# Moving the first attention step's scores and softmax into the last values chunk of the layer

## The reference

```python
def diff_attention(q, k, v, lam):
    s = jnp.einsum('bqahd,bkahd->bahqk', q, k).astype(jnp.float32) * (B_QK_DIM ** -0.5)
    p = jax.nn.softmax(s, axis=-1)
    a = (p[:, 0] - lam * p[:, 1]).astype(v.dtype)
    return jnp.einsum('bhqk,bkhe->bqhe', a, v)
```

## Time and profile before

| what | value |
|---|---|
| runs of the kernel | 3079.67 us median of 3 (3075.52 to 3081.51) |
| profiled execution | 3081.39 us, its span 3079.6 us |
| instructions | 51919 |
| TensorE matmuls | 2942.7 us busy, 96% of the span |
| TensorE weight loads | 2705.6 us, 88% |
| VectorE | 1056.2 us, 34% |
| ScalarE | 1522.4 us, 49% |
| GpSimd | 2176.1 us, 71% |
| mean granted TensorE clock | 0.966 of full speed |
| memory read, written | 488.86 MB, 3.15 MB |

### The profile page before, as it was taken

How to read it: one execution, slowest core, us unless ns; L and a number is a source line. 1 busy time by engine, 2 the same in 40 slices (tenths; PEclk the granted TensorE clock), 3 DMA queues, 4 the chain that set the end, 5 groups by cost and what they waited for, 6 DMA issues and landing times.

```text
span 3079.6 us, 51919 instructions
## 1 busy us (share of the span) xinstructions
PE 2942.7 (96%) x21842; PEld 2705.6 (88%) x21842; DVE 1056.2 (34%) x1979; ACT 1522.4 (49%) x2005; POOL 2176.1 (71%) x912
## 2 busy tenths in 40 slices
PE   7999989999999999989999999899999999999998
PEld 7877969988877879979899999787899989789998
DVE  2412422123214221031563433225634342464433
ACT  4665454446565454444564444444654444465443
POOL 6667697886667788866566886565586867557686
PEclk9999999999999999989999999899999999999999
DMA  6445455564445455544344554443354554334454
GB/s 217 144 151 171 145 196 174 185 202 154 151 151 176 159 179 185 181 156 155 134 151 158 172 179 152 163 138 112 130 167 148 178 180 157 131 124 156 149 179 147
DMA packets 136521, 495.39 MB, mean 161 GB/s; under 512 B 15072, under 2 KB 17760, under 8 KB 135136
## 3 DMA queue, kind: packets, MB, share of 16 engines
q1 hardware_dynamic: 131904, 480.53, 46.6%
q10 hardware_dynamic: 4384, 11.54, 1.1%
HBM read 488.86 MB, written 3.15 MB: 160 GB/s over the span
## 4 chain that ended last, share of the span: by engine, by line
PE 83%; ACT 6%; DVE 4%; DVEq 2%; POOL 1%; ACTq 1%; issue 1%; DMA 0%; SPq 0%
PE lin L464 17%; PE lin L465 17%; PE lin L466 17%; PE aux L464 4%; PE aux L466 4%; PE aux L465 4%; PE aux L557 2%; PE lin L490 2%; PE lin L491 2%; PE lin L492 2%; ACT whi L1003 2%; POOL wlo L443 1%; PE aux L626 1%; PE aux L898 1%; PE aux L842 1%
## 5 line engine op out<-in xcount | busy, mean ns | idle before, releaser
L443 POOL TENSOR_TENSOR wlo<-raw,whi 128x1024 fp32r<-128x1024 f32 x908 | 2175.9, 2412 | 887.9 <-ACT whi L1003 887.1
L1003 ACT ACTIVATE whi<-raw 128x1024 fp32r<-128x1024 f32 x908 | 949.6, 1057 | 982.1 <-PE lin L466 723.5
L464 PE MATMUL lin<-in_hi,whi 128*128 128x256 f32 x3968 | 1146.7, 289 | 25.2 <-POOL wlo L443 22.4
L465 PE MATMUL lin<-in_lo,whi 128*128 128x256 f32 x3968 | 1127.9, 284 | 0.0
L466 PE MATMUL lin<-in_hi,wlo 128*128 128x256 f32 x3968 | 1127.3, 284 | 0.0
L464 PEld LDWEIGHTS lin<-in_hi,whi 128*128 128x128 f32 x3968 | 766.6, 193 | 63.7 <-issue 52.8
L465 PEld LDWEIGHTS lin<-in_lo,whi 128*128 128x128 f32 x3968 | 767.0, 193 | 0.7
L466 PEld LDWEIGHTS lin<-in_hi,wlo 128*128 128x128 f32 x3968 | 766.2, 193 | 0.0
L464 PE MATMUL aux<-br_hi,whi 128*128 128x256 f32 x880 | 250.7, 285 | 7.6 <-DVE br_lo L1418 7.6
L465 PE MATMUL aux<-br_lo,whi 128*128 128x256 f32 x880 | 250.3, 284 | 0.0
L466 PE MATMUL aux<-br_hi,wlo 128*128 128x256 f32 x880 | 250.2, 284 | 0.0
(11 more groups left out here) (240 smaller groups left out, 3679.7 us busy)
## 6 DMA issues: line engine op xcount, KB each, us to landing
raw<-in_wstream SPq DMA_DIRECT2D x908, 512.0 KB, 3.3
Z<-in_rel ACTq DMA_DIRECT2D x2, 1536.0 KB, 7.1
Z<-in_mem_t ACTq DMA_DIRECT2D x2, 1024.0 KB, 7.8
kv_store<-Z ACTq DMA_DIRECT2D x2, 1024.0 KB, 7.0
Z<-kv_store ACTq DMA_DIRECT2D x2, 1024.0 KB, 11.2
x<-in_x_t SPq DMA_DIRECT2D x1, 1024.0 KB, 4.9
Z<-in_ctx_t SPq DMA_DIRECT2D x1, 1024.0 KB, 4.8
out_x<-x SPq DMA_DIRECT2D x1, 1024.0 KB, 3.9
```

Source lines behind the costliest of these rows:

```text
L443: pool.tensor_tensor(wlo[s][:, :], raw[s][:, :], whi[s][:, :].bitcast(F32), ALU.subtract).then_inc(lo_pool, 1)
L464: pe.matmul(out, wh, xh, start=start, stop=False, skip_group_check=True)
L465: pe.matmul(out, wh, xl, start=False, stop=False, skip_group_check=True)
L1003: act.activation(whi[s][:, :], raw[s][:, :], ACT.Copy).then_inc(hi_ready, 1)
```

## The change

On TensorE the scores of step 0 are issued behind the second unit (index 1) of the last values chunk, instead of after the chunk. The wait for `qk_done` goes with them. In the layer of `x` whose context keys come from memory (`stored`), they also wait for `kv_landed`, which the wait for `values_ready` covered. The wait for `values_ready` moves ahead of the first product with the values, in `diff_values(0)`. On ScalarE, lambda's two exponentials move from behind the second values chunk to behind the first, then come three of the second chunk's four conversions, the exponentials of step 0, the fourth conversion and the copy of the chunk. VectorE's program stays as it is. It applies to all three passes.

```diff
@@ diff_values (TensorE)
                 if tt == 0 and t.ahead(yb_taken, 0):
                     pe.wait_ge(yb_taken, t.ahead(yb_taken, 0))
+                if n == 0:
+                    pe.wait_ge(values_ready, t.next(values_ready))
                 pe.wait_ge(pt_ready, t.next(pt_ready))
@@ second_layer (TensorE)
-            def second_layer(kts, rotate):
+            def second_layer(kts, rotate, stored=False):
+                def first_scores():
+                    pe.wait_ge(qk_done, t.ahead(qk_done, 0))
+                    if stored:
+                        pe.wait_ge(kv_landed, t.next(kv_landed, 32))
+                    diff_scores(0, kts)
+
                 rms()
...
-                token_chunk(1)
-                pe.wait_ge(qk_done, t.ahead(qk_done, 0))
-                pe.wait_ge(values_ready, t.next(values_ready))
+                token_chunk(1, after={1: first_scores})
                 fill = second_fill()
-                diff_scores(0, kts)
                 for n in range(STEPS):
...
-            for _ in range(L):
-                second_layer(4, True)
+            for l in range(L):
+                second_layer(4, True, l == 1)
@@ second_layer (ScalarE)
                 values_chunk(0, zt(v, 4), qk_roots)
-                values_chunk(1, zt(v + 4, 4))
+                act.wait_ge(lam_sum, t.next(lam_sum))
+                act.activation(small[:, 18:20], small[:, 16:18], ACT.Exp).then_inc(lam_exp, 1)
+                hi_parts(3)
+                diff_exps(0, kts)
+                evacuate(1, 1, zt(v + 4, 4))
                 act.drain()
                 if rotate and l == 1:
                     act.wait_ge(kv_landed, t.next(kv_landed, 32))
                 act.drain().then_inc(values_ready, 1)
-                act.wait_ge(lam_sum, t.next(lam_sum))
-                act.activation(small[:, 18:20], small[:, 16:18], ACT.Exp).then_inc(lam_exp, 1)
                 fill = second_fill()
-                diff_exps(0, kts)
                 for n in range(STEPS):
```

## The result

| | time, median (range) | ratio to the kernel before, 95% interval |
|---|---|---|
| before | 3079.03 us (3073.73 to 3081.51, 5 runs) | |
| changed | 3060.53 us (3048.79 to 3068.35, 5 runs) | 0.9939 [0.9921, 0.9957] |

The change takes 18.5 us off and comes to 3060.53 us, where 3062.5 was forecast.

The account below looks back on a forecast made before the run. TensorE, busy 96%, sets the pace, so time is won only where it idles or runs at half clock. 7.4 + 8.7 + 2.7 = 18.8 us off the profiled 3081.39 gives 3062.6, taken as 3062.5; range 3056 to 3069.

Parts of the forecast that it names:

- The first gap: TensorE's idle time between the last values chunk and step 0's scores: 2.45 us in each of three passes, 7.4 removed.
- the second: TensorE's lost time between step 0's scores and its transposes: 2.31, 3.03 and 3.37 us, together 8.7 us removed.
- The clock: TensorE at half clock on scores, unit and transposes in the second pass only: 2.7 us removed.
- The added part: Cost of the new order in three queues: no stall taken; bounds nothing to 1.6 us for each 512-key pass.
- The wait for the keys and for the transfer: TensorE's early scores need the last keys, done 9.6 us earlier, and an 11.2 us transfer issued some 80 us ahead: nothing.
- Lambda's load: ScalarE's table load and exponential behind the first values chunk delay the next conversion by at most 1.5 us, covered.
- The chain: Softmax of step 0, from scores to probabilities: 6.3 us bare, ready 0.3 us before TensorE comes 9.5 us after the scores' start.
- the hold of the ratio's product: Tiny VectorE product in step 0's softmax, held by GpSimd's low-half operation from 2643.1 to 2643.7.
- A late softmax: VectorE waits under GpSimd leave part of the idle time before the transposes: at most 3.5 us, 3066; chance 0.12.
- The starving queue: ScalarE's conversion and PSUM freeing stand behind late exponentials, so TensorE waits for weights: slower, 3086; chance 0.03.
- The rival of the moved wait: Line 1346's wait is not what ended the idle time before the scores; only the later idle time goes: 3070; chance 0.03.
- The clock gave 5.65 us back: Rival: shifted idle spots downstream lose the clock more often, five new losses of 2.7 us, about 3076; chance 0.04.

Follow-up runs that it names:

- the first experiment: Kernel before with TensorE's scores right behind the whole values chunk, not waiting for the stored values, ScalarE's order unchanged: 3083.79 us against 3077.05, ratio 1.002.
- The two later comparisons: The changed kernel itself, run again against the kernel before: ratio 0.9926 (3053.89 us), then 0.9925 (3058.47 us against 3081.66).
- the placing behind the third unit: Changed kernel with the scores of step 0 behind the third unit (index 2) of the last values chunk instead of the second: 3065.58 us, one execution.
- the last experiment: Changed kernel with VectorE's fill work moved from in front of the next step's maxima to behind them: 3052.42 us, ratio 0.9895 to the kernel before.
- the other deal: Changed kernel with the second fill unit before the values moved from steps 5, 9, 13 to 4, 8, 12: 3060.24 us, ratio 0.9952 to the kernel before.

## Why the prediction was right

**The first gap, 7.4 us, and the second, 8.7.** Together 16.1 were forecast; 15.7 are gone. The sum was right, but the two terms are not independent savings, as the rival in the first experiment would have it: done one by one, the parts do not bring their terms. Moving the wait alone brought 0.0 us, moving lambda alone 2.3, moving both with the exponentials ahead of the copy, but still at the chunk's end, 5.9. The rest, 9.8 us, is the cover of two more units. The prediction did not say this; it added the gaps because the change undoes both at once. The scores at their early place with ScalarE's old order were not tried.

**The clock, 2.7 us.** By the second transposes 18.6 us are gone, so the clock's part is 2.9, of which the second pass has 2.8. The Trainium skill's rule ("TensorE: Matmul & The Clock Gate", "HAM oscillation"), that idle gaps between bursts bring back the half clock, would have given up to two more such losses. The profiled execution of before does not show them, but the runs elsewhere side with the rule more than the prediction did: the same gap at the chunk's end (2.68, 3.21, 3.55 us) lost the clock in all three passes, and with lambda alone moved the gap ahead of the scores (2.29 us) lost it in two of three. The 2.7 us thus rest on a loss that one profiled execution happened to show once; that they came out at 2.9 says that this loss is gone, and not how often the kernel before has it. The two later comparisons gave 21.9 and 23.2 us instead of 18.5; that executions of before lose the clock there more often than the one profiled did would fit, and is not shown.

**The added part, nothing.** The wait for the keys and for the transfer: no wait of line 898 in any pass. Lambda's load: in the third pass the conversion behind it came late (it starts at 2625.30, 0.7 us after its unit by the distance of the others), no TensorE wait follows. The chain: forecast ready 0.3 us before TensorE, measured 0.30; the hold of the ratio's product under GpSimd forecast to 2643.7 of the old time, 0.6 us long, measured 0.68. In the context's pass the last VectorE operation ends 0.83 us before the transposes. The rule on the shared port ("SBUF — State Buffer", "SBUF: two separate sides", of the Trainium skill) held each time. In the profile of the changed kernel 43 VectorE products on 128x1 or 128x2 numbers began inside a GpSimd operation that had over 0.2 us to run, and each ended 0.01 to 0.02 us behind it.

**The rivals.** A late softmax did not come; the placing behind the third unit shows how near it was. What the prediction held against it, that steps with two units of cover show no gap, does not hold as it stands: steps 5, 9 and 13 have two units and are the ones that wait, up to 2.88 us at step 5; the last experiment shows VectorE's backlog as a cause at step 5. The starving queue was tested and did not come. The rival of the moved wait had line 1346 not ending the first gap; the first experiment shows that it did end it, since the scores came at once without that wait, but that the time then went to the second gap. The clock gave 5.65 us back in one profiled execution, in a stretch ahead of the change, and 4.6 in another, most of it behind the attention steps; the medians of the three comparisons all show 18.5 us or more gained.

**What was thin.** The range, 3056 to 3069, held the median, but single runs of the changed kernel spread from 3048.8 to 3068.4, wider than the three runs of before had shown; a median of few runs could have fallen below it, as that of a later comparison did (3053.89).

## What to carry to other kernels

When an engine waits twice in a row, ask whether the two waits are links of one chain: if they are, take the first away alone and the second grows by as much, as it did here. A chain is shortened by reordering the engine that runs it, and covered by starting it earlier on the engine that waits; count every queue it passes, the conversion ahead of it and the holds included, and compare the sum with the cover in tenths of a microsecond. Where an engine waits inside a chain for another's result, its independent work belongs in that wait and not in front of it.

## What the runs showed of the hardware

- Half clock behind a gap went with the gap's length in most cases. At step 5 the gaps of 2.6 to 2.9 us were followed by half clock in 24 of 27 cases (nine profiles, three passes), those of 1.25 to 1.43 us in none of three; gaps of 4.2 to 5.6 us elsewhere (the wait alone, the other deal) in all six. But 3.21 us in the third pass of before was not, and 2.29 us ahead of the scores was in two of six (before and lambda alone). With 512 keys, 11.3 us pass from the transposes of step 5 to those of step 6 where the clock held (3 of 18 cases), 12.8 us in 12 cases and 14.0 in 3: behind a gap of 2.9 us the clock cost 1.5 us more in most cases, up to 2.7 in some. Two gaps of 2.3 and 2.1 us, or 2.3 and 3.2, with a unit between them cost 2.9 and 2.2 us less by the second transposes than one of 4.5 or 5.6; two of 2.3 and 2.9 cost as much as one of 5.2 (38.96 against 38.87 us).
- A VectorE product on 128x2 numbers took 0.16 us or up to 2.20 us, depending only on when GpSimd's 2.4 us operation beside it ended; passes over 128x512 that read PSUM took 0.75 us under such an operation and were not held. Three products on one column in the changed kernel's profile that began within 0.01 us of GpSimd's operation took 0.15 us: only those that came after it waited.
- The activation table load took 1.28 us each time, 91 times in each profile.
